# Fourteen weight tiles' low parts made early and kept in DRAM, and two taps per chunk moved from TensorE to VectorE

## The chip, the cores and the metric

The kernel runs on one core of a Trainium2 chip, as one program. The metric is the device time of one execution in microseconds (us), the median of three runs. PE is TensorE (the matmul engine), DVE VectorE, ACT ScalarE, POOL GpSimd and SP SyncE; SP and POOL also issue the DMAs here.

## The reference

The reference is two transformer-like blocks in a row, in fp32, on 256 latent and 256 context tokens of 1024 features. The first has a retention layer and a differential attention layer, each with a SwiGLU; the second a conformer convolution layer and an mLSTM layer, each with an MLP. Two places matter here. The first is the gate projection of the retention layer, `g` below; the second is the convolution.

```
q, k, v, g = jnp.split(h @ w_in, splits, axis=-1)          # retention; g is 2048 wide
...
return (on * jax.nn.silu(g)) @ w_out

a = u @ w_pw1 + b_pw1                                      # convolution layer, 2 x 1024 wide
a = a[..., :CONV_DIM] * jax.nn.sigmoid(a[..., CONV_DIM:])
a = dwconv(a, w_dw)                                        # 31 taps per channel, rows of 64 tokens
a = jax.nn.silu(layer_norm(a + b_dw, ln_g, ln_b))
return a @ w_pw2 + b_pw2
```

## The kernel before

Activations lie with the features on the 128 partitions and the 512 tokens along the row (8 chunks of 128 features). Every weight matrix is a stream of 620 tiles of 128 x 1024 fp32 (512 KB), in the order of the list `PHASES`; tile n goes to slot n % 4. To keep fp32 accuracy each product is made of three matmuls in a rounded format (fp32r): high x high, low x high and high x low, by `split_mm` (L798 to L800). So every weight tile passes through four steps: SP loads `w_raw` (L600); ACT rounds it to `w_hi` (L1795, through `hi_ahead`), once the tile four places before has been used; DVE subtracts, `w_lo` = `w_raw` - `w_hi` (L2551, through `lo_ahead`), and counts `w_lo_done`; PE uses it. `w_lo_done` also frees the slot of `w_raw` for SP's next load, and PE waits for it before the tile. ACT and DVE work three tiles ahead of PE (`LOOKAHEAD`). Each engine runs its own instructions in the order of the program; there is no scheduler.

The gate projection (`ret_g`, 16 tiles). PE makes the first three tiles together, then one after the other; for each tile t, ACT does `hi_ahead`, waits for PE's tile and writes silu of the bank to `ret_gate`; DVE does `lo_ahead` and scales `ret_gate` (L2872). After tile 15 ACT computes the decay exponentials of head 0 (`ret_exps`), from which DVE builds the decay (L2881 to L2884) and the masked scores (`ret_att`, L2892), which PE waits for (L1100).

The convolution stage (`pw1`, 16 tiles, then `pw2`, 8 tiles). Chunk p of 128 channels needs the tiles 2p (gate) and 2p + 1. DVE writes the gated, padded input `conv_in` (`conv_input`, three instructions, L3241 to L3245); ACT rounds it to `conv_in_hi`, DVE makes `conv_in_lo` (L3254, `conv_lo`). The 31 taps are divided: ACT makes 2, PE makes `PE_TAPS[p]` of them as matmuls with a diagonal weight (`conv_taps`, three matmuls a tap; the diagonals come from ACT, `conv_diag`), and DVE the others, one SCALAR_TENSOR_TENSOR each (L3276). DVE then adds its two sums (L3282) and PE's bank (L3286) to `conv_z`, and goes on to the next chunk. `PE_TAPS` is 14, six times 10, and 15. Between `conv_input` and `conv_lo` DVE makes the low parts of the two weight tiles that are next in line; the last of these fourteen (pw1's tiles 5 to 15 and pw2's 0 to 2) comes after the taps of chunk 7. PE's order is: tile 2p + 2, the taps of chunk p, a feature sum of an older chunk (L1347), tile 2p + 3.

`x_res` holds the residual input. In the first layer it is read by the normalization ahead of the projections (L2630) and next by the residual addition behind `ret_out` (L2667). POOL issues a few DMAs and, apart from 16 small additions for q and k, does nothing from there to the differential layer, and nothing between the memset of `conv_in` (L720) and the MLP.

Of the kernel before, what the change touches and what calls it, by code (L numbers as in the profile page):

```python
# [25 lines left out]
P = 128  # L26
# [4 lines left out]
DC = D // P  # L31
# [8 lines left out]
PE_TAPS = [14] + [10] * 6 + [15]  # L40
# [26 lines left out]
FIRST = {}  # L67
# [42 lines left out]
def _ada_at(n_tiles, n_ada, end):  # L110
# [26 lines left out]
          "lat_used": ("ada_pe_done", 1),  # L137
          "lat_std": ("ada_first0", 32),
# [5 lines left out]
          "lat_sum": ("ada_first4", 32),  # L144
          "lat_centered": ("ada_first5", 32),
# [37 lines left out]
          "xcl_spilled": ("consts_in", 32),  # L183
          "sel_in": ("decay_in", 32),
# [16 lines left out]
def program(nc, weights, ada, c_rows_d, x_t, ctx2_t, vecs_d, consts_d, ret_rope_d, ret_decay_d, diff_tab_d, lam_d,  # L201
# [9 lines left out]
    with ctx:  # L211
        base = (nc.sbuf_base + 31) // 32 * 32

        def at(name, shape, offset, dt=F32):
            return nc.alloc_sbuf_tensor_at(name, shape, dt, offset=base + offset)
# [6 lines left out]
        X = at("x_res", [P, DC, TOK], 48 * K)  # L222
        H_AT, ARENA, TMP_AT, CONST_AT = 64 * K, 96 * K, 192 * K, 202 * K
# [204 lines left out]
        c_spill = nc.dram_tensor("c_spill", (P, 4, 1024), F32).ap()  # L428
        x_spill = nc.dram_tensor("x_spill", (P, DC, TOK), F32).ap()
# [9 lines left out]
        def S(name):  # L439
            held = SHARED[name][0] if name in SHARED else name  # L440
            if held not in sems:
                sems[held] = ctx.enter_context(nc.semaphore(held))
            return sems[held]
# [225 lines left out]
        def _(pool):  # L669
# [20 lines left out]

            pool.wait_ge(S("tile_done"), FIRST["ffn0_out"] + COUNT["ffn0_out"])
# [28 lines left out]
            own(pool.memset(CIN[:, :, :], 0.0))  # L720

# [1071 lines left out]
        def _(act):  # L1793
# [173 lines left out]
            def ret_gate(t, i, s):  # L1967
                hi_ahead("ret_g", t, s)
                act.wait_ge(S("tile_done"), t + (FIRST["ret_g"] + 1))
                f(RG[:, t, :], PS[s % 8][:, :], ACT.Silu).then_inc(S("rg_free"), 1)  # L1970
# [573 lines left out]
        def _(dve):  # L2544
# [9 lines left out]
            def lo_ahead(ph, t, s):  # L2554
                n0 = FIRST[ph] + LOOKAHEAD
                lo(t + n0, (n0 + s) % SLOTS)
# [312 lines left out]
            def ret_gate(t, i, s):  # L2869
                lo_ahead("ret_g", t, s)  # L2870
                dve.wait_ge(S("rg_free"), t + 9)
                V.tensor_scalar(RG[:, t, :], RG[:, t, :], VECS[:, bass.ds(t + VEC["ret_norm_g"], 1)], None, MUL)\  # L2872
                    .then_inc(S("rg_scaled"), 1)
# [101 lines left out]
            def ffn(layer, T, q, m, x0):  # L2975
                if layer == 0:
                    rms_halves("ret_out", q, m, 0, 0, 0, 2, *mods(layer, 3))
                else:
                    inverse_std(q, T)
                    modulate(m, T, *mods(layer, 3))  # L2980
# [278 lines left out]
            for p in range(DC):  # L3259
# [6 lines left out]
                if p:  # L3266
                    lo_ahead("pw1", t - 1, t - 1)
                if 0 < p < DC - 1:
                    lo_ahead("pw1", t, t)
# [13 lines left out]
                if p == DC - 1:  # L3283
                    lo_ahead("pw1", t, t)
# [15 lines left out]
            for s in range(len(CZ_STEPS) + 2):  # L3300
                if s == OPENING:
                    cz_inverse(1)
                if s < len(CZ_STEPS):
                    c, cols = CZ_STEPS[s]
                    V.tensor_tensor(CZ[:, c, cols], CZ[:, c, cols], tmp(2)[:, cols], MUL).then_inc(S("cz_norm"), 1)
                if s >= 2:
                    c, cols = CZ_STEPS[s - 2]
                    dve.wait_ge(S("cz_hi_done"), s - 1)
                    V.tensor_tensor(HLO[:, c, cols], tmp(s % 2)[:, cols], HHI[:, c, cols].bitcast(F32), SUB)\
                        .then_inc(S("cz_lo_done"), 1)  # L3310
                if s == 8:
                    lo_ahead("pw2", 0, 0)
# [746 lines left out]
```

## Time and profile before

| | us |
|---|---|
| median of 3 runs | 3006.41 (3006.31 to 3010.77) |
| profiled execution, time | 3006.21 |
| profiled execution, span of its instructions | 3004.4 |
| PE busy | 2949.9 (98%) |
| DVE busy | 2129.7 (71%) |
| ACT busy | 1192.7 (40%) |
| POOL busy | 193.5 (6%) |

The span is divided into 40 slices in the page; the gate projection runs from about 225 to 313 us, the convolution stage from about 1250 to 1430 us. A matmul's busy time overlaps the next one's, so PE's share says little about waits shorter than a few tenths of a microsecond; starts of successive instructions are what to read.

### The profile page before, as it was taken

Reading aid. Unit: us, or ns where it says so; the run is one execution under the profiler, and the core shown is the slowest. Engines: PE = TensorE matmul, PEld = TensorE weight load, DVE = VectorE, ACT = ScalarE, POOL = GpSimd, SP = SyncE. Lnnn points to the kernel's source line nnn. Section 1 sums busy time; section 2 is a strip of 40 time slices with the busy share of each in tenths; the row PEclk is TensorE's granted clock in tenths of the full one; section 3 lists DMA queues with packets and bytes.
Section 4 is the critical chain, followed back from the end, with each engine's and each line's share of the span. In section 5 each row is a group of like instructions: output and inputs, shape, how many; then the busy total and the mean of one; then the engine's idle time right before and its main releaser. Section 6 shows DMA issues by size and latency. Waiting matters only on the chain.

```text
span 3004.4 us, 40234 instructions
## 1 busy us (share of the span) xinstructions
PE 2949.9 (98%) x14353; PEld 2420.3 (81%) x14353; DVE 2129.7 (71%) x3282; ACT 1192.7 (40%) x1803; POOL 193.5 (6%) x163
## 2 busy tenths in 40 slices
PE   7999999999999999999999999999999999999998
PEld 5888678888887789977888888788888888876787
DVE  6973688877786788699898876566754632756875
ACT  3223524332143664556441323443244422423443
POOL 2300000000001000000040210000000000002120
PEclk9999999999999999999999999999999999999999
DMA  7672065666633156311266552672366622452554
GB/s 276 200 245 92 21 197 174 215 202 240 205 102 112 57 182 222 129 57 43 99 208 212 175 183 76 213 248 100 102 219 215 215 91 92 150 188 95 199 186 144
DMA packets 125230, 479.26 MB, mean 160 GB/s; under 512 B 13752, under 2 KB 13752, under 8 KB 122768
## 3 DMA queue, kind: packets, MB, share of 16 engines
q1 hardware_dynamic: 119232, 443.60, 44.5%
q0 software_dynamic: 5840, 33.51, 3.1%
q8 instruction: 104, 1.70, 0.2%
q14 instruction: 54, 0.44, 0.0%
HBM read 459.23 MB, written 17.83 MB: 159 GB/s over the span
## 4 chain that ended last, share of the span: by engine, by line
PE 79%; issue 10%; DVE 6%; ACT 2%; DMA 1%; SPq 0%; POOL 0%; DVEq 0%; ACTq 0%; POOLq 0%
PE bank L798 21%; PE bank L800 21%; PE bank L799 21%; PE bank L811 4%; PE bank L812 2%; PE bank L1727 2%; PE bank L1100 1%; DVE x_res L2667 1%; DVE w_lo L2551 1%; PE bank L810 1%; DMA ada_first<-in_ada 1%; DVE x_res L2673 1%; PE bank L1206 1%; ACT w_hi L1795 1%; DMA ml_v<-v_spill 0%
## 5 line engine op out<-in xcount | busy, mean ns | idle before, releaser
L2551 DVE TENSOR_TENSOR w_lo<-w_raw,w_hi 128x1024 fp32r<-128x1024 f32 x617 | 754.7, 1231 | 498.1 <-ACT w_hi L1795 489.1
L1795 ACT ACTIVATE w_hi<-w_raw 128x1024 fp32r<-128x1024 f32 x620 | 649.5, 1055 | 755.6 <-PE bank L800 626.4
L798 PE MATMUL bank<-h_hi,w_hi 128*128 128x512 f32 (+1 forms) x1432 | 524.5, 366 | 7.3 <-DVE h_lo L2640 5.2
L799 PE MATMUL bank<-h_lo,w_hi 128*128 128x512 f32 (+1 forms) x1432 | 518.9, 362 | 0.0
L800 PE MATMUL bank<-h_hi,w_lo 128*128 128x512 f32 (+1 forms) x1432 | 518.8, 362 | 0.0
L798 PEld LDWEIGHTS bank<-h_hi,w_hi 128*128 128x128 f32 x1432 | 270.4, 189 | 54.9 <-issue 9.7
L799 PEld LDWEIGHTS bank<-h_lo,w_hi 128*128 128x128 f32 x1432 | 270.4, 189 | 43.7 <-issue 1.2
L800 PEld LDWEIGHTS bank<-h_hi,w_lo 128*128 128x128 f32 x1432 | 270.3, 189 | 41.6
L798 PE MATMUL bank<-w_hi,xm_hi 128*128 128x512 f32 x512 | 201.0, 393 | 0.1
L800 PE MATMUL bank<-w_hi,xm_lo 128*128 128x512 f32 x512 | 199.4, 389 | 0.0
L799 PE MATMUL bank<-w_lo,xm_hi 128*128 128x512 f32 x512 | 199.3, 389 | 0.0
L811 PE MATMUL bank<-h_hi,w_hi 128*128 128x512 f32 x532 | 191.0, 398 | 2.6 <-DVE h_hi L3412 2.2
L812 PE MATMUL bank<-h_hi,w_lo 128*128 128x256 f32 x532 | 149.3, 281 | 0.0
L729 POOL TENSOR_TENSOR mlp_lo<-tmp,mlp_hi 128x512 f32 (+1 forms) x64 | 94.7, 1480 | 556.4 <-DVE tmp L3485 457.2
L798 PE MATMUL bank<-ffn_hi,w_hi 128*128 128x256 f32 (+1 forms) x360 | 120.4, 334 | 1.7 <-issue 1.7
L811 PEld LDWEIGHTS bank<-h_hi,w_hi 128*128 128x128 f32 x532 | 100.1, 188 | 24.5 <-issue 2.2
L799 PE MATMUL bank<-ffn_lo,w_hi 128*128 128x256 f32 (+1 forms) x360 | 119.7, 332 | 0.0
L800 PE MATMUL bank<-ffn_hi,w_lo 128*128 128x256 f32 (+1 forms) x360 | 119.6, 332 | 0.0
L798 PE MATMUL bank<-w_hi,h_hi 128*128 128x512 f32 x288 | 113.6, 395 | 1.7 <-DVE w_lo L2551 1.7
L798 PEld LDWEIGHTS bank<-w_hi,xm_hi 128*128 128x128 f32 x512 | 96.2, 188 | 20.3 <-DVE x_res L3565 0.5
L800 PEld LDWEIGHTS bank<-w_hi,xm_lo 128*128 128x128 f32 x512 | 96.1, 188 | 20.1
L800 PE MATMUL bank<-w_hi,h_lo 128*128 128x512 f32 x288 | 112.2, 390 | 0.0
(473 smaller groups left out, 5667.3 us busy)
## 6 DMA issues: line engine op xcount, KB each, us to landing
w_raw<-in_weights SPq DMA_DIRECT2D x620, 512.0 KB, 4.2
ada_ring_f<-in_ada SPq DMA_DIRECT2D x56, 512.0 KB, 3.4
ada_ring_g<-in_ada SPq DMA_DIRECT2D x44, 512.0 KB, 3.4
ada_ring_b<-in_ada SPq DMA_DIRECT2D x38, 512.0 KB, 4.2
ada_ring_a<-in_ada SPq DMA_DIRECT2D x32, 512.0 KB, 3.4
ada_first<-in_ada SPq DMA_DIRECT2D x16, 512.0 KB, 15.3
v_spill<-ml_v POOLq DMA_DIRECT2D x4, 1024.0 KB, 6.9
o_spill<-ml_o_grp POOLq DMA_DIRECT2D x4, 1024.0 KB, 4.6
```

Of the source, the lines that this page charges most:

```text
L729: pool.tensor_tensor(mlo[:, t, 0:T], tmp(s % 2, T), mhi[:, t, 0:T].bitcast(F32), SUB)\
L798: mm(out, lhs[0], rhs[0], start=start, stop=False)
L799: mm(out, lhs[0], rhs[1], start=False, stop=False)
L800: return mm(out, lhs[1], rhs[0], start=False, stop=stop)
L810: return mm(bank[:, :], lhs[0], row, start=False, stop=True)
L811: mm(bank[:, :], lhs[0], row, start=start, stop=False)
L812: return mm(cross, lhs[1], row[:, 0:LAT], start=False, stop=False)
L1100: last = mm(PS[3 + t][:, :], ATT[:, a, i0:i0 + P], RV[:, v, 512 * h:512 * (h + 1)], start=n == 0, stop=n == len(keys) - 1)
L1206: mm(PS[D_SCORE[u % 2][m]][:, :], DQ[part, h, t * P:(t + 1) * P], DK[part, h, :], start=True, stop=True).then_inc(S("d_score"), 1)
L1727: last = mm(PS[6 + n % 2][:, :], MPT(h, d)[:, j, t * P:(t + 1) * P], MV2[:, j, 512 * h:512 * (h + 1)], start=i == 0, stop=i == len(keys) - 1)
L1795: return nc.scalar.activation(out, in_, func, **kw)
L2551: V.tensor_tensor(WLO[:, slot, :], RAW[:, slot, :], WHI[:, slot, :].bitcast(F32), SUB)\
```

## The change

The low parts of the fourteen weight tiles named above are made during the gate projection. They are loaded (POOL's queue) into two buffers `split_raw`, rounded by ACT to `split_hi`, subtracted by DVE to `split_lo` (in the place of `split_raw`), and stored by POOL's queue to a DRAM tensor `lo_spill`. These buffers lie on `x_res`, so `x_res` is loaded again from the input after the last store, and DVE waits for that ahead of the residual. In the convolution stage POOL loads each low part straight into its slot of `w_lo`, once the tile four places before has been used, and counts `w_lo_done` itself; `w_raw` and `w_hi` of these tiles come as before. DVE's fourteen `lo_ahead` of the stage are gone. `PE_TAPS` becomes 14, six times 8, and 15, so DVE makes 21 taps instead of 19 in the six middle chunks.

```diff
-PE_TAPS = [14] + [10] * 6 + [15]
+PE_TAPS = [14] + [8] * 6 + [15]
+N_SPLIT = 14
...
+        SRAW = at("split_raw", [P, 2, 1024], 48 * K)
+        SLO = at("split_lo", [P, 2, 1024], 48 * K, F32R)
+        SHI = at("split_hi", [P, 2, 1024], 56 * K, F32R)
...
+        lo_spill = nc.dram_tensor("lo_spill", (N_SPLIT, P, 1024), F32R).ap()
...
+            split0 = FIRST["pw1"] + LOOKAHEAD + 2
+
+            def split_load(i):
+                name = f"split_in{i % 2}"
+                pool.dma_start(SRAW[:, i % 2, :], weights[split0 + i]).then_inc(S(name), 16)
+
+            pool.wait_ge(S("h_lo_done"), DC)
+            pool.wait_ge(S("decay_in"), 32)
+            split_load(0)
+            split_load(1)
+            for i in range(N_SPLIT):
+                pool.wait_ge(S("split_lo"), N("split_lo", i + 1))
+                pool.dma_start(lo_spill[i], SLO[:, i % 2, :]).then_inc(S("split_out"), 16)
+                pool.wait_ge(S("split_out"), N("split_out", 16 * (i + 1)))
+                if i + 2 < N_SPLIT:
+                    split_load(i + 2)
+            pool.dma_start(X[:, :, :], x_t).then_inc(S("x_again"), 16)
...
+            pool.wait_ge(S("w_lo_done"), split0)
+            for i in range(N_SPLIT):
+                n = split0 + i
+                pool.wait_ge(S("tile_done"), n - LOOKAHEAD)
+                pool.dma_start(WLO[:, n % SLOTS, :], lo_spill[i]).then_inc(S("lo_in"), 16)
+                pool.wait_ge(S("w_hi_done"), n + 1)
+                pool.wait_ge(S("lo_in"), N("lo_in", 16 * (i + 1)))
+                pool.sem_inc(S("w_lo_done"), 1)
...
             def ret_gate(t, i, s):
                 hi_ahead("ret_g", t, s)
+                if t < N_SPLIT:
+                    name = f"split_in{t % 2}"
+                    act.wait_ge(S(name), N(name, 16 * (t // 2 + 1)))
+                    f(SHI[:, t % 2, :], SRAW[:, t % 2, :], ACT.Copy).then_inc(S("split_hi"), 1)
                 act.wait_ge(S("tile_done"), t + (FIRST["ret_g"] + 1))
                 f(RG[:, t, :], PS[s % 8][:, :], ACT.Silu).then_inc(S("rg_free"), 1)
...
             def ret_gate(t, i, s):
                 lo_ahead("ret_g", t, s)
+                if t < N_SPLIT:
+                    dve.wait_ge(S("split_hi"), N("split_hi", t + 1))
+                    V.tensor_tensor(SLO[:, t % 2, :], SRAW[:, t % 2, :], SHI[:, t % 2, :].bitcast(F32), SUB)\
+                        .then_inc(S("split_lo"), 1)
...
+                    dve.wait_ge(S("x_again"), N("x_again", 16))
...
-                if p:
-                    lo_ahead("pw1", t - 1, t - 1)
-                if 0 < p < DC - 1:
-                    lo_ahead("pw1", t, t)
                 conv_lo(p)
...
-                if p == DC - 1:
-                    lo_ahead("pw1", t, t)
...
                 if s == 8:
+                    dve.wait_ge(S("w_lo_done"), FIRST["pw2"] + LOOKAHEAD)
                     lo_ahead("pw2", 0, 0)
```

Some semaphores are shared with others under new offsets; that has no effect on the order.

On DVE, in the convolution stage, one middle chunk and the start of the next, before:

```order
984 L3241 SCALAR_TENSOR_TENSOR conv_in<-bank,vecs,tmp 128x8x64
985 L3242 SCALAR_TENSOR_TENSOR conv_in<-bank,vecs,tmp 128x3x15
986 L3245 SCALAR_TENSOR_TENSOR conv_in<-bank,vecs,tmp 128x3x15
987 L2551 TENSOR_TENSOR w_lo<-w_raw,w_hi 128x1024 x2
988 L3254 TENSOR_TENSOR conv_in_lo<-conv_in,conv_in_hi 128x752
989 L3276 SCALAR_TENSOR_TENSOR conv_acc<-conv_in,vecs,conv_acc 128x512 x19
990 L3282 TENSOR_TENSOR conv_acc<-conv_acc 128x512
991 L3286 TENSOR_TENSOR conv_z<-conv_acc,bank 128x512
992 L3241 SCALAR_TENSOR_TENSOR conv_in<-bank,vecs,tmp 128x8x64
```

and after:

```order
998 L3289 SCALAR_TENSOR_TENSOR conv_in<-bank,vecs,tmp 128x8x64
999 L3290 SCALAR_TENSOR_TENSOR conv_in<-bank,vecs,tmp 128x3x15
1000 L3293 SCALAR_TENSOR_TENSOR conv_in<-bank,vecs,tmp 128x3x15
1001 L3302 TENSOR_TENSOR conv_in_lo<-conv_in,conv_in_hi 128x752
1002 L3320 SCALAR_TENSOR_TENSOR conv_acc<-conv_in,vecs,conv_acc 128x512 x21
1003 L3326 TENSOR_TENSOR conv_acc<-conv_acc 128x512
1004 L3328 TENSOR_TENSOR conv_z<-conv_acc,bank 128x512
1005 L3289 SCALAR_TENSOR_TENSOR conv_in<-bank,vecs,tmp 128x8x64
```

The two `w_lo` between the input and its low part are gone, the taps went from 19 to 21, and nothing stands between the input and the low part that needs ACT's rounding of that input.

On POOL, from the q and k additions to the first DMA of the differential layer, before:

```order
14 L688 TENSOR_TENSOR ret_qk_sb<-ret_qk_sb,tmp 128x256 [waits qk_lat] x16
15 L692 DMA diff_tab<-in_diff_tab 128x512 [waits tile_done]
```

and the first rows of what stands there after (`ada_first5` is the semaphore that `split_lo` shares, `consts_in` the one of `split_out`):

```order
14 L700 TENSOR_TENSOR ret_qk_sb<-ret_qk_sb,tmp 128x256 [waits qk_lat] x16
15 L707 DMA split_raw<-in_weights 128x1024 [waits decay_in,h_lo_done]
16 L707 DMA split_raw<-in_weights 128x1024
17 L715 DMA lo_spill<-split_lo 128x1024 [waits ada_first5]
18 L707 DMA split_raw<-in_weights 128x1024 [waits consts_in]
19 L715 DMA lo_spill<-split_lo 128x1024 [waits ada_first5]
20 L707 DMA split_raw<-in_weights 128x1024 [waits consts_in]
```

A load follows each store and waits for that store to land. On ACT, the start of the gate projection, before and after:

```order
57 L1795 ACTIVATE ret_gate<-bank 128x512
58 L1795 ACTIVATE w_hi<-w_raw 128x1024
59 L1795 ACTIVATE ret_gate<-bank 128x512
60 L1795 ACTIVATE w_hi<-w_raw 128x1024
61 L1795 ACTIVATE ret_gate<-bank 128x512
```

```order
58 L1834 ACTIVATE ret_gate<-bank 128x512
59 L1834 ACTIVATE w_hi<-w_raw 128x1024
60 L1834 ACTIVATE split_hi<-split_raw 128x1024
61 L1834 ACTIVATE ret_gate<-bank 128x512
62 L1834 ACTIVATE w_hi<-w_raw 128x1024
```

Each gate tile's silu now stands behind a rounding of a split tile, and that behind the split tile's load.

## Rows read from the trace of the kernel before

**Rows 1.** The page: busy time, share, instructions by engine; the granted clock by slice.
```profile
PE 2949.9 (98%) x14353; PEld 2420.3 (81%) x14353; DVE 2129.7 (71%) x3282; ACT 1192.7 (40%) x1803; POOL 193.5 (6%) x163
PEclk9999999999999999999999999999999999999999
```

**Rows 2.** DVE's timeline, convolution: start us, us, instruction, count, [idle before <-releaser].
```profile
1261.28 0.75 DVE L3241 SCALAR_TENSOR_TENSOR conv_in<-bank,vecs,tmp 128x512 f32<-128x512 f32 x1
...
1263.34 0.94 DVE L3254 TENSOR_TENSOR conv_in_lo<-conv_in,conv_in_hi 128x752 fp32r<-128x752 f32 x1 [0.97 <-ACT conv_in_hi L1795]
1264.19 10.02 DVE L3276 SCALAR_TENSOR_TENSOR conv_acc<-conv_in,vecs,conv_acc 128x512 f32<-128x512 f32 x15
...
1275.65 0.74 DVE L3241 SCALAR_TENSOR_TENSOR conv_in<-bank,vecs,tmp 128x512 f32<-128x512 f32 x1
...
1279.05 0.94 DVE L3254 TENSOR_TENSOR conv_in_lo<-conv_in,conv_in_hi 128x752 fp32r<-128x752 f32 x1
1279.90 12.67 DVE L3276 SCALAR_TENSOR_TENSOR conv_acc<-conv_in,vecs,conv_acc 128x512 f32<-128x512 f32 x19
1292.68 0.69 DVE L3282 TENSOR_TENSOR conv_acc<-conv_acc 128x512 f32<-128x512 f32 x1
...
1294.01 0.74 DVE L3241 SCALAR_TENSOR_TENSOR conv_in<-bank,vecs,tmp 128x512 f32<-128x512 f32 x1
...
1331.19 0.75 DVE L3241 SCALAR_TENSOR_TENSOR conv_in<-bank,vecs,tmp 128x512 f32<-128x512 f32 x1 [0.38 <-PE bank L800]
...
1388.04 0.75 DVE L3241 SCALAR_TENSOR_TENSOR conv_in<-bank,vecs,tmp 128x512 f32<-128x512 f32 x1 [0.49 <-PE bank L800]
```

**Rows 3.** PE's timeline: chunk 3's first and last taps and sum, chunk 4's first.
```profile
1317.49 0.40 PE L798 MATMUL bank<-conv_in_hi,conv_diag_hi 128*128 128x512 f32 x1
...
1324.65 1.02 PE L1347 MATMUL bank<-conv_z,ones 128*128 128x512 f32 x2
...
1336.43 0.40 PE L798 MATMUL bank<-conv_in_hi,conv_diag_hi 128*128 128x512 f32 x1
```

**Rows 4.** PE's timeline: the first of chunk 7's taps.
```profile
1391.39 0.48 PE L798 MATMUL bank<-conv_in_hi,conv_diag_hi 128*128 128x512 f32 x1 [0.81 <-DVE conv_in_lo L3254]
```

**Rows 5.** ACT's timeline, gate projection: silu of tiles 1, 4 and 14, then the exponentials.
```profile
242.15 0.59 ACT L1795 ACTIVATE ret_gate<-bank 128x512 f32<-128x512 f32 x1
...
252.95 0.60 ACT L1795 ACTIVATE ret_gate<-bank 128x512 f32<-128x512 f32 x1 [3.89 <-PE bank L800]
...
307.35 0.60 ACT L1795 ACTIVATE ret_gate<-bank 128x512 f32<-128x512 f32 x1 [3.89 <-PE bank L800]
...
309.37 1.05 ACT L1795 ACTIVATE w_hi<-w_raw 128x1024 fp32r<-128x1024 f32 x1
312.79 2.56 ACT L1795 ACTIVATE ret_exp<-tmp 128x512 f32<-128x512 f32 x4 [2.38 <-PE bank L800]
```

**Rows 6.** PE's timeline behind the gate projection.
```profile
319.50 10.57 PE L1100 MATMUL bank<-ret_v_sb,ret_att 128*128 128x512 f32 x24 [0.71 <-DVE ret_att L2892]
```

**Rows 7.** DMA issues, whole span, then the gate stage's: KB each, us to landing.
```profile
w_raw<-in_weights SPq DMA_DIRECT2D x620, 512.0 KB, 4.2
o_spill<-ml_o_grp POOLq DMA_DIRECT2D x4, 1024.0 KB, 4.6
x_spill<-x_res SPq DMA_DIRECT2D x1, 2048.0 KB, 6.6
tmp<-in_ret_decay POOLq DMA_DIRECT2D x2, 512.0 KB, 4.4
ret_rope<-in_ret_rope POOLq DMA_DIRECT2D x1, 512.0 KB, 5.2
...
w_raw<-in_weights SPq DMA_DIRECT2D x16, 512.0 KB, 3.3
```

**Rows 8.** DVE and POOL side by side where POOL issued a DMA.
```profile
936.24 3.49 DVE L2551 TENSOR_TENSOR w_lo<-w_raw,w_hi 128x1024 fp32r<-128x1024 f32 x3
...
935.26 0.94 POOL L712 DMA_DIRECT2D x_res<-in_ctx_t  x1
```

More of the change, by code:

```diff
@@ L137 @@
           "lat_used": ("ada_pe_done", 1),
+          "split_in0": ("vecs_in", 32),
+          "split_in1": ("decay_in", 32),
+          "split_out": ("consts_in", 32),
+          "x_again": ("vecs_in", 144),
+          "lo_in": ("vecs_in", 160),
+          "split_hi": ("ada_first4", 32),
+          "split_lo": ("ada_first5", 32),
           "lat_std": ("ada_first0", 32),
@@ L143 @@
           "c4_hi": ("d_score", 32),
-          "lat_sum": ("ada_first4", 32),
-          "lat_centered": ("ada_first5", 32),
+          "lat_sum": ("ada_first4", 46),
+          "lat_centered": ("ada_first5", 46),
           "x_part": ("ada_first6", 32),
@@ L182 @@
           "xcl_done": ("rg_scaled", 16),
-          "xcl_spilled": ("consts_in", 32),
-          "sel_in": ("decay_in", 32),
+          "xcl_spilled": ("consts_in", 256),
+          "sel_in": ("decay_in", 144),
           "xcl_back": ("diff_tab_in", 32),
```

## The prediction

> **What bounds the kernel now.** I read the page first. PE is busy 98% of the span at full clock in all slices, DVE 71%, POOL 6% [rows 1], so the whole is paced by PE; but the change works in two stretches, and the limit has to be read there, from the starts of successive instructions, since a matmul's busy time hides short waits.
>
> In the convolution stage I set PE's period for a chunk beside DVE's. PE needs 1336.43 - 1317.49 = 18.94 us from one chunk's first tap to the next one's [rows 3]. Of this the 30 tap matmuls take 1324.65 - 1317.49 = 7.16 us, 0.239 each. DVE, from input to input, needs 1294.01 - 1275.65 = 18.36 us and shows no idle time in that chunk [rows 2]: the first middle chunks go at DVE's pace. From chunk 4 on DVE waits for PE, 0.38 to 0.5 us a chunk [rows 2]. So the two are within 0.6 us of each other, and what the change gives is set by the one that ends up longer.
>
> In the gate projection PE makes a tile in (307.35 - 252.95) / 10 = 5.44 us, and ACT waits 3.89 us of it for PE [rows 5]. There is room on ACT and DVE. Behind it the room is gone: the exponentials start at 312.79, when PE's last tile is done, and PE later waits 0.71 us for the masked scores that follow from them [rows 5, 6]. A late start of the exponentials goes into the end one for one.
>
> **PE's part of the convolution.** Six chunks lose two taps, six matmuls, each: 6 x 0.239 = 1.43 us [rows 3]. PE's period becomes 17.51 us. If PE set the pace everywhere, this would be 6 x 1.43 = 8.6 us.
>
> **DVE's part.** Two subtractions leave each middle chunk and two taps come. The taps: 19 took 12.67 us and 15 took 10.02, so one is (12.67 - 10.02) / 4 = 0.66 us and two are 1.32 [rows 2]. The subtractions do not return their whole time, because they stood where DVE otherwise waits for ACT's rounding of the chunk. Chunk 0 has none of them there and shows it: its low part starts 1263.34 - 1261.28 = 2.06 us after the input, with 0.97 us of idle time for ACT in it; in chunk 1, with the two, it starts 1279.05 - 1275.65 = 3.40 us after [rows 2]. So 1.34 us leave and 1.32 come. DVE's new period, from rows: 2.06 + 0.85 (low part) + 12.78 + 1.32 (21 taps) + 1.33 (the sums, to the next input) = 18.34 us [rows 2].
>
> 18.34 is more than PE's 17.51, so DVE sets the pace in all six chunks, and PE waits 0.8 us ahead of most chunks' taps. Inputs 1 to 7 then lie 6 x 18.34 = 110.1 us apart, against 1388.04 - 1275.65 = 112.4 before [rows 2]: 2.3 us less. In chunk 7 one subtraction stood between input and low part: PE's taps began 1391.39 - 1388.04 = 3.35 us after the input [rows 2, 4], and will do so 2.06 + 0.94 + 0.14 = 3.14 us after (0.14 is my estimate of the hand-over to PE). That is 0.2 us. The subtraction behind chunk 7's taps lay beside PE's 45 tap matmuls; it is worth nothing. ACT's 24 fewer diagonals were made in its idle time. **The stage gives 2.5 us.**
>
> **The low parts in time.** POOL loads one after the other, and each waits also for ACT's rounding. Two loads of at most 5.2 us [rows 7] a chunk of 18.3 us fit; the first is wanted some 20 us after it can start. Behind these waits POOL has only the MLP's work, and SP's load of the fourth tile after; both have more than a tile of slack. I cost this at nothing; were a low part late, PE would wait for the excess over that slack. POOL's issuing does not slow DVE: beside the issue at 935.26 three subtractions took 3.49 us, which is their ordinary 1.13 us apart [rows 8].
>
> **What the gate projection pays.** It gains 14 roundings (about 1.0 us), 14 subtractions (1.2), 14 stores and 14 loads. ACT has 3.9 and DVE as much idle time a tile, so the work is covered; the chain is not so surely. Two buffers are turned round: rounding, subtraction, store until landed, load until landed, next rounding. With about 0.4 us of hand-overs (estimate) a round takes 2.6 + S us, S being store plus load, and has 2 x 5.44 = 10.9 us. The odd buffer starts late, since the first three tiles end together: the rounding of split 1 stands where silu of tile 1 stood, at 242.15 [rows 5]. Six rounds later, split 13 is rounded at 242.15 + 6 x (2.6 + S). Behind it stand silu 13, a weight, silu 14 (2.5 us together) and then, as before, 309.37 - 307.35 + 1.05 = 3.1 us to the exponentials, wanted at 312.79 [rows 5]. So split 13 may be rounded at 307.1, which allows S = 8.2 us. Each 0.1 us more costs 0.6 us at the end. Weights feel it later: ACT's weight for tile t + 3 has two more tiles of slack.
>
> S has no row of its own, for no such store exists. Load: the nearest is `ret_decay`, same queue and size, 4.4 us; ends 3.3 (`w_raw` in this stage) and 5.2 (`ret_rope`). Store: 1024 KB took 4.6 and 2048 KB 6.6, so 512 KB would take 3.6; ends 3.3 and 4.6 [rows 7]. That makes 8.0. Now three transfers of 512 KB instead of one run in each tile's time; `w_raw` takes 3.3 us alone here and 4.2 in the median of the program, 0.9 more. The 4.4 has such company in it already; I add half of 0.9 to the store. **S = 8.4, cost 6 x 0.2 = 1.2 us**; ends S = 6.6, nothing, and 9.8, 9.6 us.
>
> The first two loads are issued some 80 us ahead of use. The reload of `x_res` (2048 KB; the store of that size took 6.6) has all of the attention and `ret_out` to land in: nothing.
>
> A page of the Trainium skill bears on S. "DMA: Bandwidth & Descriptors", section "Anatomy of one DMA", gives 2.0 us plus bytes / 436e3 for a DMA from POOL, by estimate 3.2 us each and S = 6.4, which would drop the cost of 1.2 us. The rows speak for more than this, 4.4 and 5.2 us. The same page, "SWDGE vs HWDGE vs iDMA", says that a DMA with a float32r destination always casts; all 28 transfers of low parts have such a destination, the page gives no price, and no row here has one.
>
> **Sum**, against the profiled execution's 3006.2 us (0.2 us under the median): 3006.2 - 2.5 + 1.2 = 3004.9 us.
>
> **Rivals.**
> 1. *The split chain becomes the bound* (slower). If S is above 8.2 the exponentials are late by 6 x (S - 8.2), and PE stands ahead of L1100. For it: the margin on my own rows is 0.2 us or less, and casts and company are unpriced. Against it: both transfers alone would take 3.3 to 4.4 us. S = 9.8 gives 3006.2 - 2.5 + 9.6 = 3013.3. It outweighs the gain from S = 8.6, and is slower by over 0.2% (3012.4) from S = 9.65.
> 2. *PE sets the pace, as the counts of instructions suggest*: 17.5 us a chunk. It needs DVE to be 0.8 us a chunk faster than its rows, for which the 0.97 us of idle time in chunk 0 [rows 2] would have to be unusual. It gives 3006.2 - 8.6 + 0 to 1.2 = 2998 to 2999.
> 3. *The low parts come late in the convolution, or POOL's issues hold DVE.* Fourteen issues of up to 0.94 us [rows 8] on a DVE that now sets the pace would be 13 us, less the 2.5: 3017. Rows 8 speak against it.
>
> **How the numbers follow.** The forecast, DVE's pace in the convolution and a gate cost of 0 to 4.5 us (S up to 8.95), 3003.7 to 3008.2: 0.72. Rival 1 beyond that: 0.19, of it 0.10 above 3012.4. Rival 2: 0.05. Rival 3, or a transfer far dearer than any row: 0.04. The range takes in the forecast and most of rival 1, up to its priced end, and leaves out rival 2: 3002.5 to 3013.5. About 0.2% (6 us) is what a measurement of this kernel can tell from no change. Faster by more: 0.05; slower by more: 0.10 + 0.04 = 0.14; within: 0.81.
>
> **What would show it.** DVE's inputs 18.3 us apart from chunk 1 to 7, each with about 1 us idle for ACT's rounding, and PE waiting up to 0.8 us for `conv_in_lo` a chunk. If they lie 17.5 apart, my step on the uncovered wait is wrong. In the gate stage: store and load landings that add up to S, ACT's split roundings waiting for `split_raw`, and the exponentials at 312.8 plus the cost; if they start at 312.8 the chain held. The prediction is wrong if S is beyond 6.6 to 9.8, or if DVE's taps run at another pitch than 0.66 us beside POOL's issues.

## The result and the profile after

The changed kernel takes 3019.31 us (median, 3018.37 to 3021.42), the one before 3006.55 (3006.09 to 3010.77) in the same comparison; the ratio is 1.0042, 95% interval 1.0033 to 1.0052. I had forecast 3004.9 and at most 3013.5. So it is 12.8 us slower, and rival 1, the split chain as the bound, is what happened, at more than its priced end.

The page of the changed kernel hardly shows it, as that of before hardly showed the limits [rows 1]: busy time, share and instructions by engine, then the granted clock by slice.

```profile
PE 2948.5 (98%) x14317; PEld 2415.8 (80%) x14317; DVE 2137.2 (71%) x3294; ACT 1198.4 (40%) x1793; POOL 217.7 (7%) x206
PEclk9999999999999999999999999999999999999999
```

The convolution went as worked out. DVE's timeline there (start us, us, instruction, count, idle before and releaser), to be held against [rows 2]:

```profile
1289.54 0.75 DVE L3289 SCALAR_TENSOR_TENSOR conv_in<-bank,vecs,tmp 128x512 f32<-128x512 f32 x1
...
1291.60 0.94 DVE L3302 TENSOR_TENSOR conv_in_lo<-conv_in,conv_in_hi 128x752 fp32r<-128x752 f32 x1 [0.97 <-ACT conv_in_hi L1834]
1292.46 14.00 DVE L3320 SCALAR_TENSOR_TENSOR conv_acc<-conv_in,vecs,conv_acc 128x512 f32<-128x512 f32 x21
...
1307.89 0.75 DVE L3289 SCALAR_TENSOR_TENSOR conv_in<-bank,vecs,tmp 128x512 f32<-128x512 f32 x1
...
1399.67 0.75 DVE L3289 SCALAR_TENSOR_TENSOR conv_in<-bank,vecs,tmp 128x512 f32<-128x512 f32 x1
...
1418.45 0.42 DVE L3332 TENSOR_SCALAR tmp<-bank 128x256 f32<-128x256 f32 x1 [2.33 <-PE bank L1386]
```

The inputs lie 18.35 us apart (forecast 18.34), the low part starts 2.06 us after the input with 0.97 us of idle time in it, and inputs 1 to 7 take 1399.67 - 1289.54 = 110.13 us where they took 112.39. The last row is the first subtraction of the mean, the end of the stage; before, it stood at 1405.51.

The loss is in the gate projection. ACT's timeline at its end, for [rows 5]: the last split rounding, silu of tiles 13 and 14, the exponentials.

```profile
319.23 1.06 ACT L1834 ACTIVATE split_hi<-split_raw 128x1024 fp32r<-128x1024 f32 x1 [3.79 <-DMA split_raw<-in_weights]
320.19 0.58 ACT L1834 ACTIVATE ret_gate<-bank 128x512 f32<-128x512 f32 x1
320.67 1.05 ACT L1834 ACTIVATE w_hi<-w_raw 128x1024 fp32r<-128x1024 f32 x1
321.62 0.59 ACT L1834 ACTIVATE ret_gate<-bank 128x512 f32<-128x512 f32 x1
...
323.63 1.04 ACT L1834 ACTIVATE w_hi<-w_raw 128x1024 fp32r<-128x1024 f32 x1
324.57 2.55 ACT L1834 ACTIVATE ret_exp<-tmp 128x512 f32<-128x512 f32 x4
```

The exponentials start at 324.57 instead of 312.79, straight behind ACT's own work and no longer behind PE. What the rounding waits for is its tile, which POOL loads. Three earlier roundings of the same buffer (split tiles 3, 9 and 11), then POOL's timeline, then the landings of the stage (KB each, median us from issue to landing), which answer [rows 7]:

```profile
258.87 1.06 ACT L1834 ACTIVATE split_hi<-split_raw 128x1024 fp32r<-128x1024 f32 x1 [11.15 <-DMA split_raw<-in_weights]
...
295.03 1.06 ACT L1834 ACTIVATE split_hi<-split_raw 128x1024 fp32r<-128x1024 f32 x1 [4.67 <-DMA split_raw<-in_weights]
...
307.50 1.06 ACT L1834 ACTIVATE split_hi<-split_raw 128x1024 fp32r<-128x1024 f32 x1 [4.59 <-DMA split_raw<-in_weights]
```

```profile
249.60 0.53 POOL L707 DMA_DIRECT2D split_raw<-in_weights  x1 [3.40 <-DMA lo_spill<-split_lo]
250.12 0.54 POOL L715 DMA_DIRECT2D lo_spill<-split_lo  x1
260.22 0.53 POOL L707 DMA_DIRECT2D split_raw<-in_weights  x1 [9.57 <-DMA lo_spill<-split_lo]
...
291.08 0.55 POOL L715 DMA_DIRECT2D lo_spill<-split_lo  x1
296.59 0.53 POOL L707 DMA_DIRECT2D split_raw<-in_weights  x1 [4.96 <-DMA lo_spill<-split_lo]
297.64 0.54 POOL L715 DMA_DIRECT2D lo_spill<-split_lo  x1 [0.52 <-DVE split_lo L2916]
303.02 0.53 POOL L707 DMA_DIRECT2D split_raw<-in_weights  x1 [4.84 <-DMA lo_spill<-split_lo]
303.55 0.55 POOL L715 DMA_DIRECT2D lo_spill<-split_lo  x1
```

```profile
w_raw<-in_weights SPq DMA_DIRECT2D x16, 512.0 KB, 4.8
lo_spill<-split_lo POOLq DMA_DIRECT2D x14, 512.0 KB, 4.9
split_raw<-in_weights POOLq DMA_DIRECT2D x12, 512.0 KB, 4.1
```

Two tiles cost POOL 303.55 - 291.08 = 12.47 us: four issues, two landings that it waits out, and 0.52 us for DVE. PE has 10.88 us for two tiles. The wait for a landing is written for one buffer, but it also holds the store of the other: the stores at 291.08 and 303.55 (even tiles) have no wait of their own, and DVE had ended their low parts 0.9 and 0.8 us before.

The stores of the odd tiles are held by nobody. POOL waits for DVE ahead of each of them, as for 0.52 us at 297.64, and for 0.51 to 0.73 us in all five of these rounds. So it is the odd buffer's own round that sets the pace. From rounding to rounding it takes 307.50 - 295.03 = 12.47 us: 297.64 - 295.03 = 2.61 from the rounding to the store's issue, 303.02 - 297.64 = 5.38 for the store, 307.50 - 303.02 = 4.48 for the load.

Behind it stands PE, for [rows 6], and then the clock. PE's timeline at the masked scores, and the stretches around them (us, PE, PEld, DVE, ACT, POOL busy, granted clock, DMA share, GB/s):

```profile
331.28 12.15 PE L1139 MATMUL bank<-ret_v_sb,ret_att 128*128 128x512 f32 x24 [7.89 <-DVE ret_att L2939]
```

```profile
328.00:331.30 3.30, 0.02 (x1) 0.03 (x1) 3.20 (x6) 3.26 (x6) 0.00 (x0) 0.50 0.91 384
331.30:335.00 3.70, 3.70 (x5) 1.68 (x6) 2.46 (x4) 2.97 (x4) 0.00 (x0) 0.57 0.67 282
335.00:339.00 4.00, 4.00 (x11) 1.73 (x10) 2.59 (x8) 0.76 (x2) 0.00 (x0) 1.00 0.00 0
```

PE is idle for 7.89 us; in that idle time its clock falls to the lower of its two levels (0.50 of full, 1.2 GHz), and the first 3.7 us of matmuls run at 0.57 in the mean. The same 24 matmuls took 10.57 us before and take 12.15 now, 1.58 us more. The convolution has the same on a small scale, ahead of chunk 7's taps [rows 4]:

```profile
1402.81 0.70 PE L837 MATMUL bank<-conv_in_hi,conv_diag_hi 128*128 128x512 f32 x1 [3.45 <-DVE conv_in_lo L3302]
1403.32 0.63 PE L838 MATMUL bank<-conv_in_lo,conv_diag_hi 128*128 128x512 f32 x1
```

```profile
1403.00:1407.00 4.00, 4.00 (x11) 3.10 (x12) 4.00 (x7) 2.39 (x3) 0.00 (x0) 0.59 0.01 2
1407.00:1411.00 4.00, 4.00 (x18) 3.15 (x17) 4.00 (x7) 0.00 (x0) 0.00 (x0) 1.00 0.00 0
```

Eight matmuls follow one another by 0.43 us instead of 0.24: 1.5 us lost of the stage's 2.5.

The account of the profiled executions (spans 3004.4 and 3017.6, so 13.2 us): 0.71 us of shift stand already at the rounding of split tile 1 (242.86, where silu 1 stood at 242.15), begun by a wait of PE for `h_lo` at the start of the program (5.66 us, before 5.16), ahead of the first new instruction; 11.07 more by the exponentials; 1.58 by the clock; 0.5 until the convolution's first input, which I did not trace; 0.94 back in the convolution (2.26 + 0.21 - 1.5); 0.3 in the rest.

### The profile page after: what moved, and what is told of

Its sections match the earlier page's. It is cut to its first block, busy times and chain, and to the rows that moved or that the text cites. A ratio compares the mean times of both kernels' runs of the same rounds, so it can differ in the third digit from the quotient of the medians.

```text
span 3017.6 us, 40226 instructions
## 1 busy us (share of the span) xinstructions
PE 2948.5 (98%) x14317; PEld 2415.8 (80%) x14317; DVE 2137.2 (71%) x3294; ACT 1198.4 (40%) x1793; POOL 217.7 (7%) x206
## 4 chain that ended last, share of the span: by engine, by line
PE 73%; DVE 10%; issue 10%; DMA 3%; ACT 3%; POOL 0%; SPq 0%; DVEq 0%; ACTq 0%; POOLq 0%
PE bank L837 19%; PE bank L838 19%; PE bank L839 19%; PE bank L850 4%; DVE conv_acc L3320 3%; PE bank L851 2%; PE bank L1766 2%; DMA split_raw<-in_weights 1%; PE bank L1139 1%; DMA lo_spill<-split_lo 1%; DVE x_res L2710 1%; DVE w_lo L2594 1%; PE bank L849 1%; ACT w_hi L1834 1%; DMA ada_first<-in_ada 1%
## 5 line engine op out<-in xcount | busy, mean ns | idle before, releaser
L2594 DVE TENSOR_TENSOR w_lo<-w_raw,w_hi 128x1024 fp32r<-128x1024 f32 x603 | 737.9, 1231 | 490.6 <-ACT w_hi L1834 481.8
```

The costliest lines, as they stand in the source:

```text
L2594: V.tensor_tensor(WLO[:, slot, :], RAW[:, slot, :], WHI[:, slot, :].bitcast(F32), SUB)\
```

## The experiments

The first question was which half of the change does what.

```diff
-PE_TAPS = [14] + [8] * 6 + [15]
+PE_TAPS = [14] + [10] * 6 + [15]
```

> The changed kernel with PE_TAPS back at 14, six times 10, 15; the low parts still come from DRAM. It tells the two halves of the change apart. Theory: the loss of 13.9 us ahead of the convolution is the gate projection's alone and stays. In the convolution DVE would need 18.35 - 1.32 = 17.0 us a chunk and PE 18.94, so PE sets the pace: DVE's inputs 1 to 7 lie about 6 x 18.94 = 113.6 us apart (before 112.4, changed kernel 110.1). PE has no long idle time ahead of chunk 7's taps, so the 1.5 us that the fall of the clock costs there comes back. Sum against the changed kernel: +3.5 - 1.5 = about +2 us, some 3021 us. Rival: the gain of the stage comes from the low parts that left DVE and not from the taps; then the inputs lie 110 us apart or less and the time is 3018 us.

Measured: 3020.02 us, ratio to before 1.0049 (1.0032 to 1.0065), so the changed kernel's time to within the runs' spread. PE waits the same 7.89 us for the masked scores. The inputs settle at 18.94 us apart with DVE now waiting 1.8 us a chunk for PE: the gain in pace comes from the taps. The first step was shorter than I said (1287.64 to 1304.79), since DVE had to catch up, so the seven inputs take 111.9 us and not 113.6. Chunk 7's taps begin after 0.60 us of idle time at full clock. So the two taps bring 1.75 us in pace and lose 1.5 of it again through the clock.

The next two take the buffers apart from POOL's queue. Both have three buffers `split_raw`/`split_lo` and one `split_hi`. Of POOL's loop, in the first:

```diff
+                pool.wait_ge(S("split_lo"), N("split_lo", i + 1))
+                if i:
+                    pool.wait_ge(S("split_out"), N("split_out", 16 * i))
+                    if i + 2 < N_SPLIT:
+                        split_load(i + 2)
+                pool.dma_start(lo_spill[i], SLO[:, i % 3, :]).then_inc(S("split_out"), 16)
```

> The changed kernel with three buffers of split_raw and one of split_hi in the same 16 KB a partition, and POOL waiting for a store only when the next low part is ready, ahead of issuing that one, so that a wait for a landing holds nothing. All theories in which the chain of stores and loads makes the loss (too large S in a buffer's round; POOL's queue held by the wait) expect the exponentials within 1 us of before's 312.8, PE's wait ahead of the masked scores back at about 0.7 us, and full clock behind it. The stage then costs nothing, and with the convolution as in the changed kernel (0.9 us less than before) the time is 3005.6 us, ratio to before 0.9997, 13.5 us under the changed kernel. Rival: the loss is the work itself (28 more transfers and 28 more instructions make weights or silu late); then the exponentials stay 3 us or more behind 312.8 and the time is above 3009 us.

and in the second:

```diff
+                pool.wait_ge(S("split_lo"), N("split_lo", i + 1))
+                pool.dma_start(lo_spill[i], SLO[:, i % 3, :]).then_inc(S("split_out"), 16)
+                pool.wait_ge(S("split_out"), N("split_out", 16 * (i + 1)))
+                if i + 3 < N_SPLIT:
+                    split_load(i + 3)
```

> Three buffers as in the run beside it, but POOL waits for each store to land before it does anything else, as in the changed kernel. It tells a buffer's round from POOL's queue. Theory of POOL's queue: a tile costs POOL two issues (0.54 + 0.53) and one landing (about 4.9), 6.0 us against the 5.44 in which PE makes one, whatever the number of buffers; POOL's last stores go back to back, the rounding of the last split tile falls at about 309, and the exponentials are 1.5 to 5 us later than 312.8, the time 3007 to 3011 us. Theory of the buffer's round (2.6 + S = 11.6 us against 10.9): three buffers have 16.3 us, so the exponentials are on time and the time is that of the run beside it, 3005.6 us.

Measured: 3013.07 us (1.0017, 1.0007 to 1.0027) and 3013.09 (1.0018, 1.0008 to 1.0028). My expectation for the first was wrong by 7.5 us, and its timeline says why. For the second, the theory of POOL's queue found the mechanism but priced it too low (3007 to 3011 us). POOL, with three buffers, first kernel and then second:

```profile
284.30 0.53 POOL L708 DMA_DIRECT2D split_raw<-in_weights  x1 [5.06 <-DMA lo_spill<-split_lo]
284.82 0.54 POOL L721 DMA_DIRECT2D lo_spill<-split_lo  x1
290.56 0.53 POOL L708 DMA_DIRECT2D split_raw<-in_weights  x1 [5.20 <-DMA lo_spill<-split_lo]
291.08 0.55 POOL L721 DMA_DIRECT2D lo_spill<-split_lo  x1
```

```profile
293.26 0.53 POOL L708 DMA_DIRECT2D split_raw<-in_weights  x1 [5.48 <-DMA lo_spill<-split_lo]
293.78 0.54 POOL L717 DMA_DIRECT2D lo_spill<-split_lo  x1
299.28 0.53 POOL L708 DMA_DIRECT2D split_raw<-in_weights  x1 [4.96 <-DMA lo_spill<-split_lo]
299.80 0.54 POOL L717 DMA_DIRECT2D lo_spill<-split_lo  x1
```

In both POOL does not wait for DVE any more once the stage is under way, and still needs 6.26 and 6.02 us for the tile shown, 6.3 and 6.5 in the mean of nine and eight tiles: two issues and one landing. I had only moved the wait, not taken it out: with one store in flight at a time a landing is in every tile's cycle. A third buffer takes the round of a buffer out (16.3 us where about 12 are needed), so what is left is POOL's queue. It does not quicken the pace: from split tile 3 to 13 the first of them needs 6.30 us a tile, the changed kernel 6.04. That these kernels are 6 us faster comes from the start, where the rounding of split tile 3 stands at 251.20 in the first of them and at 258.87 in the changed kernel, and that of tile 4 at 257.67 in the second and at 264.01 in the changed kernel.

My prediction had no price for the type of the low parts. The next run asks whether it makes the transfers slow.

```diff
-        lo_spill = nc.dram_tensor("lo_spill", (N_SPLIT, P, 1024), F32R).ap()
+        lo_spill = nc.dram_tensor("lo_spill", (N_SPLIT, P, 1024), F32).ap()
...
-                pool.dma_start(lo_spill[i], SLO[:, i % 2, :]).then_inc(S("split_out"), 16)
+                pool.dma_start(lo_spill[i], SLO[:, i % 2, :].bitcast(F32)).then_inc(S("split_out"), 16)
...
-                pool.dma_start(WLO[:, n % SLOTS, :], lo_spill[i]).then_inc(S("lo_in"), 16)
+                pool.dma_start(WLO[:, n % SLOTS, :].bitcast(F32), lo_spill[i]).then_inc(S("lo_in"), 16)
```

> The changed kernel with lo_spill declared float32 and both ends of the 28 transfers of low parts taken as float32, so that none has a float32r end; nothing else moves. Theory that the type makes the store slow: the landing of lo_spill falls from 4.9 to about 3.6 us, a tile costs POOL 4.7 us, less than 5.44, and the exponentials come at 313 to 316, the time 3006 to 3010 us. Rival: the type costs nothing and the store takes 4.9 us because three transfers share the engines; then landing, exponentials (324.6) and time (3019 us) are those of the changed kernel within 1.5 us.

Measured: 3021.32 us (1.0042, 1.0029 to 1.0054); landings of 4.9 us for the stores and 4.2 for the loads of `w_lo` in the convolution; the changed kernel has 4.9 and 4.3. The type costs nothing that can be seen here. In the profiled execution the exponentials came at 328.04, 3.5 us later than in the changed kernel and not within the 1.5 us that the rival allowed; ACT waited 7.40 us for one load there, and for the others behind the first round 2.4 to 5.6.

What does cost, then, is company. In the changed kernel the first two stores and the last land in 3.6, 3.7 and 3.2 us; those between, but for one, in 4.5 to 5.2. In the next kernel the split loads from the third on are left out (ACT and DVE split what lies in the buffer), with the stores and their waits as they were.

```diff
-                if i + 2 < N_SPLIT:
-                    split_load(i + 2)
```

> The changed kernel without its split loads from the third on: ACT and DVE split what lies in the buffer instead (so the low parts are not those of the weights), with the same stores and the same waits for them. It tells what makes a store land in 4.9 us instead of 3.5 to 3.9, which the first two and the last show. Theory: the load that is issued 0.5 to 1.1 us before or after it on the same queue; without it the store lands in 3.5 to 3.9 us beside w_raw, POOL needs under 5 us a tile, and the exponentials come at 313. Rival: w_raw on SP's queue is enough company, the landing stays at 4.7 us or more.

```profile
w_raw<-in_weights SPq DMA_DIRECT2D x17, 512.0 KB, 4.0
lo_spill<-split_lo POOLq DMA_DIRECT2D x14, 512.0 KB, 3.7
```

The stores land in 3.7 us in the median (2.9 to 5.6, and one of 6.9), the exponentials are back behind PE's last tile, and the time of the one run is 3007.88 us. So by this execution a store is worth the 3.6 us that I took for it, and the split load on the same queue makes it 4.9.

One store lands late here too, so the long landings in the changed kernel are not the loads' doing alone. The load issued at 249.60 landed after 9.3 us and the store at 250.12 after 9.8, and a `w_raw` issued beside them after 9.0. At the same place a split load took 9.1 us in the run with the plain type and 9.0 in the second three-buffer run, so this is not the chance of one execution. Weight loads crowd there, since three tiles end together. But in the changed kernel the DMA engines are busy for 0.38 of the time from 256 to 258 us and 0.22 of it from there to 259.9, so full engines are not all of the cause. It stays open.

Now the wait itself, in the run called e5. Three buffers, and a semaphore for the even and one for the odd stores, so that the store waited for is the one before:

```diff
+                pool.wait_ge(S("split_lo"), N("split_lo", i + 1))
+                pool.dma_start(lo_spill[i], SLO[:, i % 3, :]).then_inc(S(f"split_out{i % 2}"), 16)
+                if i:
+                    name = f"split_out{(i - 1) % 2}"
+                    pool.wait_ge(S(name), N(name, 16 * ((i - 1) // 2 + 1)))
+                    if i + 2 < N_SPLIT:
+                        split_load(i + 2)
```

> Three buffers again, but now two stores may be in flight, each counted on a semaphore of its own: POOL issues store i as soon as the low part is there, then waits for store i - 1 and loads tile i + 2. The two runs before had POOL wait for one landing a tile (5.2 us) beside two issues (0.54 each), 6.3 us a tile, with any number of buffers. Theory that this wait in POOL's queue is what is left: store i - 1 is 5.4 us old when it is waited for, POOL has about 4 us of idle time a tile for the next low part, split roundings come 5.44 us apart, the exponentials at 312.8 to 314, PE's wait ahead of the masked scores is about 0.7 us; time 3004 to 3006 us, about 7.5 us under the three-buffer runs. Rival: three transfers of 512 KB a tile are more than the queues move in 5.44 us; then landings grow beyond 6 us, the roundings stay more than 6 us apart and the time stays near 3013 us.

Measured: 3006.29 us, ratio to before 0.9995 (0.9986 to 1.0005). POOL and PE:

```profile
280.89 0.53 POOL L718 DMA_DIRECT2D lo_spill<-split_lo  x1 [4.08 <-DVE split_lo L2924]
281.42 0.54 POOL L709 DMA_DIRECT2D split_raw<-in_weights  x1
285.52 0.53 POOL L718 DMA_DIRECT2D lo_spill<-split_lo  x1 [3.56 <-DVE split_lo L2924]
286.04 0.54 POOL L709 DMA_DIRECT2D split_raw<-in_weights  x1
```

```profile
321.24 10.57 PE L1145 MATMUL bank<-ret_v_sb,ret_att 128*128 128x512 f32 x24 [0.71 <-DVE ret_att L2947]
```

POOL waits for DVE again, PE for 0.71 us, and the 24 matmuls take their old 10.57. The gate projection now costs nothing, with the same 28 transfers and 28 instructions in it. The rival, that the transfers are too many, is out, though the landings moved (medians of the gate stage): the load that now stands behind the store takes 6.8 us and the store 3.9, where it was 4.1 and 4.9. The sum is larger (10.7 against 9.0) and harmless: three buffers have 16.3 us for a round, and POOL waits for a landing only when the store is a tile old. Two stores in flight with only two buffers were not run.

In this profile the clock fell longer ahead of chunk 7: from its input to the subtraction of the mean 1407.39 - 1387.41 = 19.98 us, against 18.78 in the changed kernel and 1414.08 - 1396.83 = 17.25 in the second three-buffer kernel, where the idle time ahead of the taps was the same 3.44 us and the clock stayed full. Two runs filled that idle time, with 18 small matmuls and with 11 instead of 4:

```diff
-                    turn_over(6 if p == 0 else 4, conv_bank(p))
+                    turn_over(6 if p == 0 else 18, conv_bank(p))
```

> As e5_two_stores, but in PE's 3.4 us of idle time ahead of chunk 7's taps 14 more small matmuls (128x256, 0.25 us each) on ones and vecs fill the bank that the taps overwrite. In the changed kernel, and in one of the two three-buffer runs, the granted clock fell to its lower level for some 3.5 us behind that idle time, 1.5 us lost; in the other it did not. Theory: without the idle time the clock stays full in every run, chunk 7's input to the subtraction of the mean takes 17.25 us and not 18.75, and the median is up to 1.5 us under e5_two_stores. Rival: the fillers delay the taps or the clock falls for another reason; then the same or slower.

> e6_two_stores_warm had its fillers mis-sized: one of them takes two passes, 7.93 / 18 = 0.44 us, so 18 took 7.9 us where 1.89 + 3.44 = 5.3 us were free, and the taps of chunk 7 began 2.3 us late, at full clock. Here there are 11 (about 4.9 us), 0.5 us short of the free time. Theory: the clock stays full and the taps begin when the low part is there: from chunk 7's input to the subtraction of the mean 17.25 us (e5: 19.98 with the clock down, e6: 19.61), so 2.7 us under a run of e5 in which the clock fell; median between that of e5 (some of its runs may have kept the clock) and 2.7 us below it, 3003.6 to 3006 us. Rival: the clock falls without an idle stretch ahead of it; then 18.75 to 20 us again and the time of e5.

Measured: 3006.69 us (0.9998, 0.9989 to 1.0007) and 3005.14 (0.9993, 0.9984 to 1.0003). I had priced a filler at half of what it takes; 18 delayed the taps, as the rival said. With 11, PE's timeline (each filler shows as two matmuls):

```profile
1383.94 4.91 PE L868 MATMUL bank<-vecs,ones 128*128 128x256 f32 x22
...
1389.27 0.47 PE L843 MATMUL bank<-conv_in_hi,conv_diag_hi 128*128 128x512 f32 x1 [0.43 <-DVE conv_in_lo L3310]
```

The taps start on time at full clock, and the stretch takes 1403.38 - 1386.13 = 17.25 us, 2.7 less than in the profile of e5. That the fillers kept the clock is not shown by it: the second three-buffer kernel kept it in its profile without them. In the medians it is 1.15 us, less than the runs' spread.

Last, what the prediction named as the reason why DVE keeps the pace: its uncovered wait for ACT's rounding. On top of e5's kernel, the input of chunk p + 1 goes ahead of the sums of chunk p:

```diff
+                if p + 1 < DC:
+                    next_input(p + 1)
                 dve.wait_ge(S("dve_own"), own.at)
                 own(V.tensor_tensor(acc0, acc0, acc1, ADD))
```

> As e5_two_stores, and in the convolution DVE makes the input of chunk p + 1 straight after the taps of chunk p, ahead of the two sums of chunk p (1.33 us); so ACT rounds the input beside the sums, and DVE's 0.97 us of idle time a chunk is covered. Theory that this uncovered wait is what kept DVE at 18.35 us: its period becomes 17.4 us, PE with 17.51 sets the pace, inputs 1 to 7 lie about 105.1 us apart (changed kernel 110.1), and PE's idle time ahead of chunk 7 shrinks below 2.5 us. Sum: e5_two_stores less 5.0 for the six chunks and about 1 us for the earlier start: 2998 to 3000 us. Rival: the sums were not what ACT needed covered (ACT's own queue, or PE's bank that comes free later) and DVE stays above 18 us; then the time is that of e5_two_stores, about 3005 us.

Measured: 2998.34 us (2996.90 to 2998.69), ratio to before 0.9969 (0.9957 to 0.9981). DVE's timeline:

```profile
1326.96 0.69 DVE L3339 TENSOR_TENSOR conv_acc<-conv_acc 128x512 f32<-128x512 f32 x1
1327.68 0.69 DVE L3341 TENSOR_TENSOR conv_z<-conv_acc,bank 128x512 f32<-128x512 f32 x1
1328.29 0.94 DVE L3310 TENSOR_TENSOR conv_in_lo<-conv_in,conv_in_hi 128x752 fp32r<-128x752 f32 x1
1329.14 14.00 DVE L3331 SCALAR_TENSOR_TENSOR conv_acc<-conv_in,vecs,conv_acc 128x512 f32<-128x512 f32 x21
1343.37 0.75 DVE L3297 SCALAR_TENSOR_TENSOR conv_in<-bank,vecs,tmp 128x512 f32<-128x512 f32 x1 [0.22 <-DVE conv_acc L3331]
```

The low part has no wait, the inputs lie 17.5 us apart, which is PE's period of rival 2, and PE waits for `conv_in_lo` in two places only, 1.05 us of it ahead of chunk 7, where its clock stays full. Held against the profile of e5, inputs 1 to 7 take 104.9 us instead of 110.1, the step from input 0 to 1 12.9 instead of 14.4, and chunk 7 to the subtraction of the mean 17.65 instead of 19.98, where the clock had fallen. This version is 8.9 us faster than the kernel before in the same comparison; by the medians it is 8 us faster than e5 and 21 us faster than the changed kernel.

## Why the prediction was wrong

**Convolution, held.** The period (18.34 forecast, 18.35 measured), the 0.97 us that come back as idle time, chunk 7's taps 3.14 us after the input (3.14), the low parts in time (PE waits for none of them in the stage), POOL's issues beside DVE (21 taps in 14.00 us, 0.667 each): each as worked out. What I left out is that PE, once DVE sets the pace, stands idle 3.45 us ahead of chunk 7, where no tile lies between, and may lose its clock: 1.5 us of the 2.5. I had written that PE waits "up to 0.8 us"; for chunk 7 PE's order gives more, since one weight tile fewer stands ahead of its taps than ahead of the others, and only 1.89 us of small matmuls in its place.

**Gate projection, S = 8.4: that is the step that failed.** The mechanism was the one I had worked out and named as rival 1: two buffers turned round, and "a round takes 2.6 + S". Each of the odd buffer's last five rounds is 2.61 or 2.62 us plus its store and its load. Timed from the issue to the instruction that waits, S was 8.99, 9.43, 9.89, 9.86 and 9.12 us, and 13.2 in the first round (3.9 and 9.3). I had 8.4 for all six, with ends of 6.6 and 9.8. The difference is 4.8 us in the first round and 5.3 in the other five, and the first round's other part took 2.8 instead of 2.6. Six rounds at S = 8.4 make 66.0 us; they took 319.23 - 242.86 = 76.4. With the way from there to the exponentials 0.5 us shorter than in my sum, this turns the cost of 1.2 us into the 11.07 measured at the exponentials.

Within S it was the store. The loads of the five rounds took 4.24 to 4.50 us, as the 4.4 that I took; the stores 4.75 to 5.42 (4.5 to 5.1 to the landing, and some 0.3 until POOL went on, which my 0.4 us for all hand-overs did not cover), where I had 4.05. I had added half of 0.9 for company; the split load on its own queue costs 1.2 (4.9 against 3.7 without it). The medians of the table, 4.9 + 4.1 = 9.0, would give 6 x 0.8 = 4.8 us only: they leave out these 0.3 us, the odd buffer's loads land in 4.2 to 4.5 and the even one's in 3.8 to 3.9, and a median leaves out the 9.3.

I had also priced the store from the cheapest row of each size. Beside the 6.6 us of `x_spill` stand `c_spill` with 9.3 and `z_spill` with 10.0, and beside the 4.6 of `o_spill` this row of the kernel before, on the same queue:

```profile
v_spill<-ml_v POOLq DMA_DIRECT2D x4, 1024.0 KB, 6.9
```

**POOL's queue, a second limit that I left out.** The two buffers share POOL, which runs in order, and a landing that it waits out is a busy time of its queue. A tile costs it 0.53 us for the load's issue, the store's landing, and some 0.3 us until it goes on; that has to be under 5.44 us, so the landing under about 4.6. The stores between the first two and the last took 4.5 to 5.2, and one 9.8. In the changed kernel this limit stands 0.5 us a round behind the buffer's, as POOL's waits for DVE show. With a third buffer it is the limit, 6.3 and 6.5 us a tile and 3013 us; so a third buffer alone would not have made the stage free. I asked what is behind POOL's waits in the convolution stage and did not ask it in the gate stage.

**What follows a late stage.** I let a late start go into the end one for one. It was 1.58 us more, because in PE's wait of 7.89 us the granted clock fell to 0.50. The loss does not follow the length of the wait: behind waits of 7.88, 6.74 and 5.84 us, in the three-buffer runs and the one with the plain type, the same 24 matmuls took 12.9, 13.0 and 13.25 us, 2.3 to 2.7 more than at full clock.

**The whole difference.** The profiled execution took 3019.4 us, 14.5 more than the 3004.9 forecast: 9.9 from the cost of the gate stage (11.07 for 1.2), 1.6 from the clock behind it, 1.6 from the convolution (0.94 for 2.5, by the clock at chunk 7), and 1.5 from the shift at the start and the parts that were not traced.

**The two rules that were weighed.** "DMA: Bandwidth & Descriptors", section "Anatomy of one DMA", of the Trainium skill gave S = 6.4 by estimate; its 3.2 us for one transfer is met by the last store of the changed kernel (3.2) and nearly by the first two (3.6, 3.7), but in company the two made 9.0 by the medians, and the measurement decides. Section "SWDGE vs HWDGE vs iDMA" of the same page of the Trainium skill says that a float32r destination always casts; taken as float32 the same 28 transfers land in 4.9 and 4.2 us, as before in 4.9 and 4.3, so here that has no price.

## What to carry to other kernels

Price a chain of DMAs twice: once for each buffer, and once for the queue that issues and waits, where every landing that is waited for in order is a busy time of that queue; more buffers do not help the second. Where an engine's work is moved away to make another one the bound, look at the wait that the moved work stood in, and at what else could stand there: here the sums of the chunk before were worth 8 us, where the forecast gave the whole change 1.3. A chain of twelve transfers that stands 0.2 us a round from its limit has no margin, since one late landing is never made good; price such a chain with the transfers that will run beside it, and not as six times a median.

## What was not expected

- Two transfers issued back to back on POOL's queue: the first lands about as if alone (store 3.9 us), the second late (load 6.8); with the order turned it was the load 4.1 to 4.6 and the store 4.9 to 5.2 (medians).
- The same idle time of 3.44 us ahead of the same instruction left the clock full in one execution and took it to its lower level for 1.5 us of loss in another and 2.7 in a third. Such a loss is a spread, not a constant.
- Splitting fourteen tiles more in the gate projection costs PE nothing once the waits are right, although ACT and DVE do 28 more instructions there and the weights' landing goes from 3.3 to 6.2 us.
